# The three split-float products of a tile, moved from two matmuls of 512 and 256 columns to three of 256 that accumulate in one place of PSUM

## What is computed

```python
def conv_ffn(h, w_up, conv_w, conv_b, w_down):
    z = h @ w_up                                   # 2048 -> 2*5632
    zp = jnp.pad(z, ((0, 0), (CONV_W - 1, 0), (0, 0)))
    z = conv_b + sum(conv_w[k] * zp[:, k:k + T] for k in range(CONV_W))   # 3 taps, causal
    a, v = jnp.split(z, 2, axis=-1)
    return (jax.nn.silu(a) * v) @ w_down

def chunked_sgu(h, w_in, v_gain, w_s, b_s, w_out):
    u, v = jnp.split(jax.nn.gelu(h @ w_in), 2, axis=-1)
    ...
    return (u * sv) @ w_out
# layer 0: x += g1 * chunked_sgu(modulate(x)); x += g2 * conv_ffn(modulate(x))
# one shared set of keys and values from x (the compressed ones through a small MLP)
# layer 1: x += g1 * nsa_attention(...);       x += g2 * conv_ffn(modulate(x))
```

## Time and profile before

| what | value |
|---|---|
| time, median of 3 runs | 2696.38 us (2695.71 to 2696.85) |
| span of the profiled execution | 2699.8 us, first to last instruction |
| PE busy, matmuls | 2556.0 us (95%), 13984 instructions |
| DVE, ACT, POOL busy | 2120.2 us (79%), 1237.2 us (46%), 454.1 us (17%) |
| mean granted TensorE clock | 0.973 of full speed |

### The profile page before, as it was taken

The page is one execution under the profiler, slowest core; times in us unless marked ns, Lnnn a source line. Parts: engine busy times, 40 slices in busy tenths (PEclk is TensorE's granted clock), DMA queues, the critical chain, the costliest instruction groups (busy, mean ns, idle before and its releaser), DMA issues.

```text
span 2699.8 us, 38453 instructions
## 1 busy us (share of the span) xinstructions
PE 2556.0 (95%) x13984; PEld 2192.4 (81%) x13984; DVE 2120.2 (79%) x2557; ACT 1237.2 (46%) x1638; POOL 454.1 (17%) x229
## 2 busy tenths in 40 slices
PE   3789999998999999999998999999899999999998
PEld 2568888887888888888887889788788888888887
DVE  6967898899888878887789896687987756665665
ACT  2254443444544345534544444483454535453543
POOL 4000110233112011200132400172212101110110
PEclk9899999999999999999999998898999999999999
DMA  7979688886777876787665877406677654555443
GB/s 291 386 305 351 243 324 326 324 325 233 280 267 280 331 263 260 268 316 287 257 237 225 323 279 295 182 2 234 246 280 270 239 193 176 190 193 184 178 178 133
DMA packets 94310, 685.47 MB, mean 254 GB/s; under 512 B 10465, under 2 KB 10465, under 8 KB 11233
## 3 DMA queue, kind: packets, MB, share of 16 engines
q1 hardware_dynamic: 93746, 681.27, 66.7%
q10 hardware_dynamic: 432, 2.38, 0.2%
HBM read 681.51 MB, written 2.10 MB: 253 GB/s over the span
## 4 chain that ended last, share of the span: by engine, by line
PE 74%; DVE 12%; DMA 6%; issue 3%; ACT 3%; POOL 2%; ACTq 0%; DVEq 0%; SPq 0%; POOLq 0%
PE banks L1393 42%; PE banks L1395 21%; DMA raw<-in_stream 6%; DVE w_lo L1034 4%; DVE raw L1050 3%; PE banks L1362 2%; PE banks L1364 2%; PE banks L1365 2%; ACT w_hi L883 1%; PE banks L755 1%; DVE zpad L1130 1%; DVE temp L1098 1%; DVE temp L1140 1%; PE banks L719 1%; PE banks L741 1%
## 5 line engine op out<-in xcount | busy, mean ns | idle before, releaser
L1393 PE MATMUL banks<-h_op,w_hi 128*128 128x512 f32 x3840 | 1373.4, 402 | 42.6 <-DVE w_lo L1034 23.2
L1034 DVE TENSOR_TENSOR w_lo<-raw,w_hi 128x1024 fp32r<-128x1024 f32 x841 | 1072.8, 1300 | 425.4 <-ACT w_hi L883 421.6
L883 ACT ACTIVATE w_hi<-raw 128x1024 fp32r<-128x1024 f32 x841 | 870.5, 1054 | 982.1 <-PE banks L1395 580.8
L1395 PE MATMUL banks<-h_op,w_lo 128*128 128x256 f32 x3840 | 1085.7, 283 | 0.0
L1393 PEld LDWEIGHTS banks<-h_op,w_hi 128*128 128x128 f32 x3840 | 730.8, 190 | 227.1 <-DVE w_lo L1034 27.1
L1393 PE MATMUL banks<-act_op,w_hi 128*128 128x512 f32 x2176 | 772.6, 399 | 11.6 <-POOL act_op L1258 6.8
L1395 PEld LDWEIGHTS banks<-h_op,w_lo 128*128 128x128 f32 x3840 | 735.2, 191 | 0.1
L1395 PE MATMUL banks<-act_op,w_lo 128*128 128x256 f32 x2176 | 613.0, 282 | 0.0
L1050 DVE CUSTOM_DVE_ANT_0 raw<-raw,c_all 128x2048 f32<-128x2048 f32 x224 | 559.1, 2517 | 13.1 <-ACT c_all L869 9.6
L1393 PEld LDWEIGHTS banks<-act_op,w_hi 128*128 128x128 f32 x2176 | 411.4, 189 | 113.9 <-issue 8.4
L1395 PEld LDWEIGHTS banks<-act_op,w_lo 128*128 128x128 f32 x2176 | 414.0, 190 | 0.0
(11 more groups left out here) (149 smaller groups left out, 1392.8 us busy)
## 6 DMA issues: line engine op xcount, KB each, us to landing
raw<-in_stream SPq DMA_DIRECT2D x645, 1024.0 KB, 5.5
x_res<-in_x SPq DMA_DIRECT2D x1, 2048.0 KB, 11.2
out_x<-x_res SPq DMA_DIRECT2D x4, 512.0 KB, 5.1
mix_area<-in_w_s ACTq DMA_DIRECT2D x1, 1024.0 KB, 4.9
mix_area<-in_b_s ACTq DMA_DIRECT2D x1, 1024.0 KB, 8.2
small<-in_small SPq DMA_DIRECT2D x1, 682.0 KB, 16.2
attn_area<-in_pos ACTq DMA_DIRECT2D x1, 273.0 KB, 5.5
c_all<-in_c SPq DMA_DIRECT2D x1, 8.0 KB
```

What stands on the lines that cost most here:

```text
L883: act.activation(w_hi[:, out, 0:n], raw[:, slot, half:half + n], ACT.Copy).then_inc(hi_ready, 1)
L1034: dve.tensor_tensor(w_lo[:, out, 0:n], raw[:, slot, half:half + n], w_hi[:, out, 0:n].bitcast(F32), ALU.subtract).then_inc(stream, 2 if ch ...
L1393: pe.matmul(banks[:, g + j, :], hi[:, k, P * j:P * (j + 1)], operand[:, kt, :], start=(kt == 0), stop=False, skip_group_check=True)
L1395: last = pe.matmul(banks[:, g + j, 0:T], lo[:, k, P * j:P * (j + 1)], operand[:, kt, 0:T], start=False, stop=(kt == last_kt), skip_group_c ...
```

## The change

Each pair of matmuls, `w_hi` against high and low part together (512 columns, into the whole bank) and `w_lo` against the high part (256 columns), becomes three matmuls of 256 columns, all into columns 0:256. Nothing has to be added afterwards, so the `zpad` copy and the add are gone: ACT and DVE make the taps straight from PSUM in stage 0, the activations of `u`, `cmp` and `gate` read PSUM, and a `dn` chunk has 4 updates for 8. The group of a `ua`/`uv` chunk is released after the taps (`conv`), no longer after the add.

```diff
@@ PE
-                                pe.matmul(banks[:, g + j, :], hi[:, k, P * j:P * (j + 1)], operand[:, kt, :],
-                                          start=(kt == 0), stop=False, skip_group_check=True)
-                                last = pe.matmul(banks[:, g + j, 0:T], lo[:, k, P * j:P * (j + 1)],
-                                                 operand[:, kt, 0:T], start=False, stop=(kt == last_kt),
-                                                 skip_group_check=True)
+                                out, a_hi, a_lo = tile_psum(g, j), operand[:, kt, 0:T], operand[:, kt, T:HILO]
+
+                                pe.matmul(out, hi[:, k, P * j:P * (j + 1)], a_hi, start=(kt == 0),
+                                          stop=False, skip_group_check=True)
+                                pe.matmul(out, hi[:, k, P * j:P * (j + 1)], a_lo, start=False, stop=False,
+                                          skip_group_check=True)
+                                last = pe.matmul(out, lo[:, k, P * j:P * (j + 1)], a_hi, start=False,
+                                                 stop=(kt == last_kt), skip_group_check=True)
...
@@ PE, cmp (gate alike)
-                            pe.matmul(banks[:, g + i, 0:2 * NB], hi[:, k, :], rows, start=(row == 0), stop=False,
-                                      skip_group_check=True)
+                            pe.matmul(banks[:, g + i, 0:NB], hi[:, k, :], rows[:, 0:NB], start=(row == 0),
+                                      stop=False, skip_group_check=True)
+                            pe.matmul(banks[:, g + i, 0:NB], hi[:, k, :], rows[:, NB:2 * NB], start=False,
+                                      stop=False, skip_group_check=True)
...
@@ ACT
-                if e == 1 and kind in ("ua", "uv"):
-                    act.wait_ge(zsum, prev.val(lambda c: c.n["zsum"] + 1))
+                if e == 0 and kind in ("ua", "uv"):
+                    done_wait(act, prev)
                     act.wait_ge(alo, prev.val(lambda c: c.n["alo"]))
                     act.wait_ge(gated, prev.val(lambda c: c.n["gated"]))
                     for j in range(TPC):
-                        act.activation(y4[:, j, :], zpad[:, j, 2:T + 2], ACT.Identity, bias=conv_col(prev, None, j),
+                        act.activation(y4[:, j, :], tile_psum(g, j), ACT.Identity, bias=conv_col(prev, None, j),
                                        scale=conv_col(prev, 2, j)).then_inc(tap2, 1)
...
@@ DVE
-                    dve.tensor_tensor(out, src, out, ALU.add).then_inc(zsum, 1)
-                if e == 1 and kind in ("ua", "uv"):
-                    dve.wait_ge(zeroed, 1)
+                if e == 0 and kind in ("ua", "uv"):
                     for j in range(TPC):
                         dve.wait_ge(tap2, prev.val(lambda c: TPC * c.n["tap2"]) + j + 1)
                         dve.scalar_tensor_tensor(
-                            out=y4[:, j, :], in0=zpad[:, j, 1:1 + T], scalar=conv_col(prev, 1, j),
-                            in1=y4[:, j, :], op0=ALU.mult, op1=ALU.add).then_inc(tap1, 1)
+                            out=y4[:, j, 1:T], in0=tile_psum(g, j)[:, 0:T - 1], scalar=conv_col(prev, 1, j),
+                            in1=y4[:, j, 1:T], op0=ALU.mult, op1=ALU.add).then_inc(tap1, 1)
...
-                    for part, j in UPDATES["all" if whole else e]:
-                        if part:
-                            dve.wait_ge(xup, TPC * n + j + 1)
-                        elif j < TPC - 1:
+                    for j in UPDATES["all" if whole else e]:
+                        if j < TPC - 1:
```

More of the change, by code:

```diff
@@ L187, in plan @@
             count["c"] += 1
-            if k in ("ua", "uv", "u", "kvf", "q", "cmp", "gate"):
-                count["zlo"] += 1
-                count["zsum"] += 1
+            if k in ("kvf", "q"):
+                count["zread"] += 1
             if k in ("ua", "uv"):
@@ L219, in free_rule @@
     if ch.kind == "dn":
-        return "xlow", TPC * (ch.n["xup"] + 1)
-    return "zsum", ch.n["zsum"] + 1
+        return "xup", TPC * (ch.n["xup"] + 1)
+    if ch.kind in ("ua", "uv"):
+        return "conv", ch.n["conv"] + 1
+    if ch.kind == "u":
+        return "gated", ch.n["gated"] + 1
+    if ch.kind == "cmp":
+        return "cmp_gelu", 1
+    if ch.kind == "gate":
+        return "gates_ready", 1
+    return "zread", ch.n["zread"] + 1
 class At:
@@ L264 @@
 ORDER = {ch.n["c"]: ch for ch in EVERY}
+ORDER_Q = {ch.loc: ch for ch in EVERY if ch.kind == "q"}
 def build(nc, io, stop=None):
@@ L479, in done_wait @@
             eng.wait_ge(sub_done, prev.val(lambda c: c.n["S"] + c.nsub))
-        UPDATES = {0: [(0, j) for j in range(TPC)], 1: [(1, j) for j in range(TPC)],
-                   "all": [(0, 0), (0, 1), (1, 0), (0, 2), (1, 1), (0, 3), (1, 2), (1, 3)]}
+        UPDATES = {0: (0, 1), 1: (2, 3), "all": range(TPC)}
         def h_tiles(e):
@@ L939, in evacuate @@
                     act.activation(gt, y, ACT.Silu).then_inc(gated, 1)
-                if e == 1 and kind == "u":
-                    act.wait_ge(zsum, prev.val(lambda c: c.n["zsum"] + 1))
-                    act.activation(gt, y, ACT.Gelu_apprx_tanh).then_inc(gated, 1)
+                if e == 0 and kind == "u":
+                    done_wait(act, prev)
+                    act.wait_ge(prod, prev.val(lambda c: c.n["prod"]))
+                    act.activation(gt4, tiles4, ACT.Gelu_apprx_tanh).then_inc(gated, 1)
                 if e == 3 and kind in ("uv", "u"):
@@ L945, in evacuate @@
                     act.activation(act_tiles(prev)[:, :, 0:T], y4, ACT.Copy).then_inc(ahi, 1)
-                if e == 1 and kind == "cmp":
-                    act.wait_ge(zsum, prev.val(lambda c: c.n["zsum"] + 1))
-                    act.activation(cmp_g[:, :], cmp_g[:, :], ACT.Gelu_apprx_tanh).then_inc(cmp_gelu, 1)
                 if e == 2 and kind == "cmp":
+                    act.wait_ge(zread, BY_NAME["kv"][-2].n["zread"] + 1)
                     act.activation(squares[:, 4096:6144], scratch[:, 4096:6144], ACT.Square).then_inc(keys_squared, 1)
@@ L1160, in evacuate @@
                         dve.scalar_tensor_tensor(
-                            out=x[:, kt, :], in0=banks[:, g + j, T * part:T * (part + 1)], scalar=vec(gate, kt),
-                            in1=x[:, kt, :], op0=ALU.mult, op1=ALU.add).then_inc(xlow if part else xup, 1)
+                            out=x[:, kt, :], in0=tile_psum(g, j), scalar=vec(gate, kt),
+                            in1=x[:, kt, :], op0=ALU.mult, op1=ALU.add).then_inc(xup, 1)
                 if e == 3 and first and name == "sgu_u0":
```

77 lines of the change are left out of this document (30 added, 47 removed).

## The result

The changed kernel takes 2705.97 us (median of 12 runs, 2702.73 to 2710.71), the kernel before beside it 2696.75 us (12 runs, 2693.36 to 2702.66). The ratio is 1.003, 95% interval 1.0017 to 1.0043: slower by 0.3%, 5 to 12 us. The forecast was 2653 us, with a chance of 0.69 for faster and 0.21 for slower. The time lies in the range (2605 to 2718), near the rival with 2713.

The account below looks back on a forecast made before the run. PE was taken as the bound, busy 95% of the span, by matmul pace and waits. Terms -30 - 14 - 5.6 + 13 - 6 = -43 us took the 2699.8 us span to 2657, median 2653 us; range 2605 to 2718.

Parts of the forecast that it names:

- the rival with 2713: The rival that each matmul costs its columns plus a constant, paid three times per tile and step: 2713 us, chance 0.25.
- The pace of three matmuls of 256: At 6016 places on PE, three 256-column matmuls take 0.350 to 0.352 us against 0.352 for a pair: 6 us gained.
- a fixed cost per matmul: Rival: on PE, a constant beside the columns makes three matmuls 0.361 us at 6016 places; 2713 us, chance 0.25.
- The load or the columns alone set the pace: Rival, faster still: on PE three matmuls take 0.340 us at 6016 places; 2587 us, chance 0.10.
- The waits behind `uv`: PE's waits for `w_lo` and `act_op` after `uv` chunks mostly go, without copy and add: 25 + 5 = 30 us gained.
- The falls of the clock: Drops of PE's clock to 1.2 GHz behind the waits, 1.6 us each, nine of ten gone: 14 us gained.
- The `cmp` chunk: In the chunk with 120 and 60 columns, a third matmul costs a third weight load: 13 us lost, between 7 and 18.
- The updates: Residual updates, four for eight: 4 us ahead of renormalisations and 1.6 us at the program's end, 5.6 us gained.
- the other gains: What the terms besides the pace save together; said to be used up at 0.359 us for three matmuls.
- the case far above: Rival: three loads and streams on PE disturb each other, 0.379 us or more for three; 2813 us, chance 0.04.
- The rule of the Trainium skill: N / 2.4 GHz plus about 2.5 ns per warm matmul; alone, one more per pair costs 15 us, giving 2673 us.

## Why the prediction was wrong

**The step that failed** is "The pace of three matmuls of 256", where I took "0.350 to 0.352, since it is the direct distance from one start to the next". It is 0.360. The term was set at a gain of 6 us; measured it is a loss of (0.360 - 0.352) by 6016, 48 us. That alone turns -43 us into +11, and the result is +9.

Two readings led there. The distance behind a 256-column matmul is 0.117 in a pair, but a pair is periodic over 768 columns, and how its time is divided between its two starts says nothing about a chain of another period. And I read the gate chunk (0.345 us with loads of 48 columns) as proof "that this isn't the load's doing", beside 0.347 to 0.353. The difference of 2 to 8 ns is exactly what was at stake, 12 to 48 us over 6016 places, and I called it "hardly less". The versions with narrower loads show that the width of the load changes the pace: 768 columns take 0.340 us with loads of 64 columns, in two matmuls or in three. Beside a 256-column stream a full load makes a matmul 0.0069 us longer than one of 64 columns does (0.1199 - 0.1130), one of 96 columns 0.0034.

How a load comes to cost that is not shown. On 0.340 us one such addition makes 0.347 and two make 0.353, the two paces of the pair, and three make 0.360; but this is arithmetic and not a mechanism. 512 columns after 512 with full loads take 0.227, just what 0.340 - 0.113 leaves for them, so there the full load adds nothing; no single pair takes 0.353; with half loads there are 508 sets of three at 0.360; and the pairs of the gate chunk took 0.345, not 0.340, with loads narrower still. What puts a stretch at one pace or the other was not found. The 0.352 that the prediction took for the pair holds: it is the mean over the 5886 undisturbed pairs in the trace of the kernel before.

**The rival "a fixed cost per matmul"** gave the right number (0.361) by the wrong mechanism: the cost changes with the width of the load. With a fixed cost all half loads would have run at 0.120, not one in twelve, and 96 columns too; and the pair with half loads would have kept its 0.347. Its arithmetic (pair less a 512) was sound since it took away what a whole matmul with its load adds. At 0.25 it should have stood first: it rested on sums over whole periods, the forecast on one distance within a period.

**"The load or the columns alone set the pace"**: 0.340 is real, but with half a load (in most of that run), not with a full one.

**The waits behind `uv`** (25 + 5 us) were right, and the mechanism was too: the chain moved as a whole, and of 34.8 us about 2 remain. It moved by 6.2 us where 2.7 were expected, and the half of that which is POOL's shorter product is luck: no row pointed to it. The two `act_op` waits of 3.4 us, of which 2.7 each were to go, went entirely. That ACT's order is what makes the waits is shown by the version that changes the order alone and takes 21 us of `w_lo` waits away. **The falls of the clock** behind them (14 us) went too, as far as the stages show it: both FFN stages stand at 1.00 for 0.98 and 0.99.

**The `cmp` chunk** was right: +13 us expected, 13.6 us between the medians, 14 us in the two traces. **The updates**, 5.6 us, weren't tested alone. The trace shows four updates in 1.66 us for eight in 3.23 at the first of the three places, as forecast, and one at the end:

```profile
653.82 1.66 DVE L1144 SCALAR_TENSOR_TENSOR x_res<-banks,mod_sums,x_res 128x256 f32<-128x256 f32 x4
...
2704.02 0.48 DVE L1144 SCALAR_TENSOR_TENSOR x_res<-banks,mod_sums,x_res 128x256 f32<-128x256 f32 x1 [0.23 <-PE banks L1388]
```

**The sum**: the spans differ by 7.8 us. With +48 for the pace and +14 for `cmp`, what is left for the gains is 54 us, by subtraction; 30 + 14 + 5.6 were forecast. Three small sums of the prediction are off, and nothing hangs on them: the other gains, 36.6 us, are used up at 0.358 us for three and not at 0.359; the case far above is 2821 us, since the 6 us gained go with it; and a cost of 15 us for 6 gained gives 2675 us and not 2673.

**The rule of the Trainium skill** that was weighed (TensorE: Matmul & The Clock Gate, Back-to-back issue gap) has a constant of 2.5 ns per warm matmul; with it the time would have been some 2675 us. The direction that it gave, that cutting a matmul costs, was right where mine was wrong; the size is 8 ns here (0.360 - 0.352), and the narrower loads show that it isn't a constant of the matmul.

## What to carry to other kernels

When a tile's products are regrouped into more matmuls, count the weight loads before the columns: price a sequence by sums over whole periods at the width of load that it will have, and treat a few ns as a result when they stand at six thousand places. In these runs a full load added nothing where 512 moving columns follow 512, cost 7 ns more than a half load at 256 in most of the run, and set the pace at 224 and below. And look whether the waits that a change would remove can be had from the order of one engine alone: one letter moved in each of two patterns brought 1.2%, and in one pattern alone 1.1%, where the large change, which removed the same waits and more, made the kernel 0.3% slower.

## What the hardware showed unexpectedly

The start-to-start distance of 256-column float32r matmuls at the higher clock: 0.113 us with loads of 64 columns, but 0.120 in some 180 us of the same run, 0.1164 with 96, 0.1199 with 128, and 0.1114 for 224 columns with a full load. Full loads with few columns behind them follow each other at 0.111 to 0.112 (60 columns in `cmp`, 128 in the earlier trace rows).

The clock: in the kernel before, PE fell to 1.2 GHz behind ten of fifteen waits of some 1.9 us or more: eight of the thirteen for `w_lo`, both for `act_op`. In the version with three matmuls apart the thirteen were 1.6 us, PE's loads filled more of the time between them (92% of the span for 81%), and behind all thirteen the clock stayed at 1.00. Which of the two held it up was not tried.

POOL's product of two 128x1024 tiles took 6.56 us where DVE ran splits and a conditioning sum beside it, 3.25 us in the changed kernel. In exchange DVE's three splits beside it took 5.70 us there, where two took 2.35 before; who waits for whom is not shown.
